# The third channel tile of a depthwise convolution, multiplied on ACT and added on POOL in turns with the fourth

## What is computed

```python
def causal_dwconv(u_ext, w, b):
    C = u_ext.shape[-1]
    y = lax.conv_general_dilated(u_ext, w[:, None, :], (1,), 'VALID',
                                 dimension_numbers=('NWC', 'WIO', 'NWC'), feature_group_count=C)
    return y + b

def conformer_conv(u, hist, conv_w, conv_b, ln_g, ln_b):
    ext = jnp.concatenate([hist, u], 1)
    y = jax.nn.silu(layernorm(causal_dwconv(ext, conv_w, conv_b), ln_g, ln_b))
    return y, ext[:, -(CONV_WIDTH - 1):]
```

## Time and profile before

| | before |
|---|---|
| median of 3 runs | 1135.22 us (1134.2 to 1147.78) |
| profiled execution, its own span | 1129.5 us |
| PE busy | 1068.1 us (95%) |
| DVE busy | 584.4 us (52%) |
| ACT busy | 395.1 us (35%) |
| POOL busy | 198.6 us (18%) |
| L1077 on DVE, 180 taps | 114.7 us |
| L638 on POOL, 30 adds | 50.3 us |

### The profile page before, as it was taken

How to read it: one execution, slowest core, us unless ns; L and a number is a source line. 1 busy time by engine, 2 the same in 40 slices (tenths; PEclk the granted TensorE clock), 3 DMA queues, 4 the chain that set the end, 5 groups by cost and what they waited for, 6 DMA issues and landing times.

```text
span 1129.5 us, 18024 instructions
## 1 busy us (share of the span) xinstructions
PE 1068.1 (95%) x6757; PEld 933.5 (83%) x6757; DVE 584.4 (52%) x1109; ACT 395.1 (35%) x683; POOL 198.6 (18%) x274
## 2 busy tenths in 40 slices
PE   4999966999999999999999969999999999999996
PEld 2999966767776667999998749999999999777774
DVE  4359599955543444233332274666666666311224
ACT  5111363332221313233221263455545554321212
POOL 6342364322221210001011000111111111000000
PEclk9999987899995955999999968999999999999998
DMA  6665332110000000223235301323222222332222
GB/s 191 156 181 168 67 66 60 57 34 2 1 1 1 1 1 1 76 74 93 74 92 160 105 19 57 92 75 92 74 86 81 87 80 74 93 84 80 75 75 84
DMA packets 110745, 83.93 MB, mean 74 GB/s; under 512 B 12962, under 2 KB 97834, under 8 KB 110632
## 3 DMA queue, kind: packets, MB, share of 16 engines
q1 hardware_dynamic: 104368, 65.64, 20.5%
q0 software_dynamic: 3904, 14.66, 4.7%
q10 hardware_dynamic: 2426, 2.98, 0.9%
HBM read 78.19 MB, written 7.18 MB: 76 GB/s over the span
## 4 chain that ended last, share of the span: by engine, by line
PE 87%; DVE 6%; DMA 2%; ACT 2%; issue 1%; POOL 1%; POOLq 0%; DVEq 0%; SPq 0%; ACTq 0%
PE ps L1405 21%; PE ps L1407 21%; PE ps L1406 21%; DVE yc L1077 4%; PE ps L1629 4%; PE ps L1472 3%; PE ps L1579 3%; PE ps L1610 2%; PE ps L1437 2%; PE ps L1582 2%; PE ps L1641 1%; PE ps L1627 1%; DMA page<-in_state_kv_win_dram 1%; PE ps L1584 1%; DMA x<-in_x_sample_dram 1%
## 5 line engine op out<-in xcount | busy, mean ns | idle before, releaser
L1405 PE MATMUL ps<-zh,wh 128*128 128x288 f32 (+1 forms) x1264 | 380.3, 301 | 21.5 <-DVE wl L1011 19.5
L1407 PE MATMUL ps<-zh,wl 128*128 128x288 f32 (+1 forms) x1264 | 378.1, 299 | 0.0
L1406 PE MATMUL ps<-zl,wh 128*128 128x288 f32 (+1 forms) x1264 | 378.1, 299 | 0.0
L1405 PEld LDWEIGHTS ps<-zh,wh 128*128 128x128 f32 (+1 forms) x1264 | 240.9, 191 | 23.6 <-DVE wl L1011 20.2
L1406 PEld LDWEIGHTS ps<-zl,wh 128*128 128x128 f32 (+1 forms) x1264 | 241.0, 191 | 0.9
L1407 PEld LDWEIGHTS ps<-zh,wl 128*128 128x128 f32 (+1 forms) x1264 | 240.6, 190 | 0.9
L1011 DVE TENSOR_TENSOR wl<-raw,wh 128x1024 fp32r<-128x1024 f32 (+1 forms) x49 | 59.1, 1205 | 183.9 <-ACT wh L706 183.6
L706 ACT CAST wh<-raw 128x1024 fp32r<-128x1024 f32 (+1 forms) x49 | 50.7, 1034 | 270.6 <-PE ps L1407 246.6
L1077 DVE SCALAR_TENSOR_TENSOR yc<-ext,par,yc 128x64 f32<-128x64 f32 (+1 forms) x180 | 114.7, 711 | 0.0
L968 ACT CAST wh<-raw 128x1024 fp32r<-128x1024 f32 x44 | 46.1, 1047 | 139.6 <-PE ps L1407 139.6
L849 ACT ACTIVATE probs<-ps,nmax 128x512 f32<-128x512 f32 (+5 forms) x76 | 39.4, 518 | 144.7 <-DVE nmax L1152 144.5
(11 more groups left out here) (256 smaller groups left out, 1605.8 us busy)
## 6 DMA issues: line engine op xcount, KB each, us to landing
raw<-in_w_up_dram SPq DMA_DIRECT2D x44, 512.0 KB, 3.9
raw<-in_w_in_dram SPq DMA_DIRECT2D x30, 512.0 KB, 3.9
raw<-in_w_down_dram SPq DMA_DIRECT2D x22, 512.0 KB, 3.8
page<-in_cache_kv_dram POOLq DMA_DIRECT2D x16, 256.0 KB, 3.0
raw<-in_w_out_dram SPq DMA_DIRECT2D x8, 512.0 KB, 3.8
x<-in_x_prompt_dram SPq DMA_DIRECT2D x4, 512.0 KB, 5.5
page<-in_state_kv_win_dram POOLq DMA_DIRECT2D x16, 128.0 KB, 2.9
raw<-in_w_in_dram SPq DMA_DIRECT2D x8, 256.0 KB, 3.5
```

Of the source, the lines that this page charges most:

```text
L1405: nc.tensor.matmul(out, ah, bh, start=start, stop=False)
L1406: nc.tensor.matmul(out, ah, bl, start=False, stop=False)
L1407: return nc.tensor.matmul(out, al, bh, start=False, stop=stop)
```

## The change

Tile 2 (the third) leaves DVE. ACT now makes, for each tap `l`, the product of tile 2 and then of tile 3, and POOL adds them in the same order. A product and its add have the number t = 2(l - 1) + h with h = 0 for tile 2 and 1 for tile 3, and take place t % 4 of the ring. One semaphore, `conv_23`, counts the adds of both. A product waits from t = 4 on until t - 3 adds are done, which frees its place. An add waits for its product and until t - 1 adds are done: with two tiles in turns that is the last add into its own tile, not the add straight before. DVE's tiles 0 and 1 keep their steps.

```diff
             for l in range(1, CW):
-                pool.wait_ge(conv_prod, 2 * (l + 1))
-                if l > 1:
-                    pool.wait_ge(conv_3, l - 1)
-                nc.gpsimd.tensor_tensor(yc[:, CT - 1, :], yc[:, CT - 1, :], cprod[:, l % 4, :], ALU.add)\
-                    .then_inc(conv_3, 1)
+                for h, c in enumerate((CT - 2, CT - 1)):
+                    t = 2 * (l - 1) + h
+                    pool.wait_ge(conv_prod, 2 * (2 * l + h + 1))
+                    if l > 1:
+                        pool.wait_ge(conv_23, t - 1)
+                    nc.gpsimd.tensor_tensor(yc[:, c, :], yc[:, c, :], cprod[:, t % 4, :], ALU.add)\
+                        .then_inc(conv_23, 1)
...
-                    if l >= 5:
-                        act.wait_ge(conv_3, l - 4)
-                    for part in range(2):
-                        w, src, dst = tap(CT - 1, l, part)
-                        if l == 0:
-                            nc.scalar.activation(dst, src, ACT.Identity, bias=par[:, P_CB + CT - 1:P_CB + CT],
-                                                 scale=w).then_inc(conv_prod, 1)
-                            continue
-                        prod = cprod[:, l % 4, 0:SEQ] if part == 0 \
-                            else cprod[:, l % 4, SEQ:NT].rearrange("p (b t) -> p b t", t=DT)
-                        nc.scalar.activation(prod, src, ACT.Copy, scale=w).then_inc(conv_prod, 1)
+                    for h, c in enumerate((CT - 2, CT - 1)):
+                        t = 2 * (l - 1) + h
+                        if t >= 4:
+                            act.wait_ge(conv_23, t - 3)
+                        for part in range(2):
+                            w, src, dst = tap(c, l, part)
+                            if l == 0:
+                                nc.scalar.activation(dst, src, ACT.Identity, bias=par[:, P_CB + c:P_CB + c + 1],
+                                                     scale=w).then_inc(conv_prod, 1)
+                                continue
+                            prod = cprod[:, t % 4, 0:SEQ] if part == 0 \
+                                else cprod[:, t % 4, SEQ:NT].rearrange("p (b t) -> p b t", t=DT)
+                            nc.scalar.activation(prod, src, ACT.Copy, scale=w).then_inc(conv_prod, 1)
...
-            act.wait_ge(conv_3, CW - 1)
+            act.wait_ge(conv_23, 2 * (CW - 1))
...
-                for done, tiles in ((conv_01, (0, 1)), (conv_2, (2,))):
-                    s0 = S_GLU + 2 * (tiles[-1] + 1)
-                    if s0 <= s < S_GATE:
-                        conv_taps(done, tiles, CW * (s - s0) // (S_GATE - s0), CW * (s + 1 - s0) // (S_GATE - s0))
+                s0 = S_GLU + 4
+                if s0 <= s < S_GATE:
+                    conv_taps(conv_01, (0, 1), CW * (s - s0) // (S_GATE - s0), CW * (s + 1 - s0) // (S_GATE - s0))
...
                             pe.wait_ge(conv_01, 4 * CW)
-                            pe.wait_ge(conv_2, 2 * CW)
-                            pe.wait_ge(conv_3, CW - 1)
+                            pe.wait_ge(conv_23, 2 * (CW - 1))
```

More of the change, by code:

```diff
@@ L321, in build_layer @@
         conv_01 = sem("conv_01")
-        conv_2 = sem("conv_2")
-        conv_3 = sem("conv_3")
+        conv_23 = sem("conv_23")
         conv_prod = sem("conv_prod")
```

## The result

| | before | changed |
|---|---|---|
| median | 1135.84 us (4 runs) | 1160.95 us (4 runs) |
| ratio | 1 | 1.0179, 95% interval 1.0104 to 1.0253 |
| the same again, in a later session | 1137.08 us (16 runs) | 1158.42 us (6 runs), ratio 1.022 (1.017 to 1.027) |
| profiled execution, span | 1129.5 us | 1155.5 us |
| L1520 / L1522 starts (compressed scores) | 205.53 us | 230.07 us |

The medians are over all runs, but the ratios and their intervals leave out the runs in a slower state of the chip, in which a program now and then finds itself (here one of the changed kernel's four, 1196.58 us). The changed kernel is slower, by 20 us by the ratio, 25 us between the medians and 26.0 us between the profiled spans. 32.6 were forecast. The measured ratio lies at the edge of 2%: the second, narrower interval is 1.7% to 2.7%.

What follows compares the result with a forecast made beforehand. PE bounds the kernel through L1520's start, which POOL's adds would set: 133.0 + 100.8 (56 adds at 1.80) + 2.5 + 1.8 = 238.1 us, 32.6 later. So 1135.2 + 32.6 = 1168 us, range 1151 to 1177.

Steps and rivals of the forecast that it cites:

- What bounds the kernel: Whole chain: mostly PE, with DVE in the convolution stretch; whatever moves L1520's start moves the end, with no later slack.
- DVE isn't relieved: Convolution from 128.9 us: 42 taps fewer save DVE 19 us, 30 more adds cost it 32 us.
- POOL becomes the bound, by the ring of four: Convolution stretch: ACT's last product waits for 56 adds, holding up the `ktok` copy and L1520; 14.4 us a step.
- The sum: First add to L1520: 144.5 + 52c for c us an add, so 238.1 us, + 32.6 us.
- First add: Start of POOL's adds: 131.8 us before, plus one more ACT pair of 1.15 us, gives 133.0.
- The hole: Step 12: ACT is away 9.7 us, four adds cover 7.2, so POOL is empty for 2.5 us.
- The pace: POOL's adds beside DVE's taps: 1.80 us an add, gap of 0.14 left in; 56 adds take 100.8 us.
- The last pair and the copy: End of the convolution: last pair 0.97 us, `ktok` copy to L1520 0.92, less 0.1 overlap, 1.8 us.
- The chances: Whole kernel: slower by over 2% 0.85, within 2% 0.12, faster 0.03.
- Rival A: POOL's adds run at nearly their own pace, 1.40 to 1.60 us; 1147 to 1157 us; chance 0.12.
- Rival B: DVE's relief decides: PE's 19.5 us of waiting come back, the kernel gets faster, 1116 us; chance 0.03.
- Rival C: DVE and POOL take turns by whole instructions: 2.01 us an add, + 44, 1179 us; chance 0.10 including beyond the main case.

Runs made afterwards that it cites:

- the trial with the relief alone: Kernel before, with the third tile's 42 DVE taps from step 10 on left out and nothing in their place; 1120.59 us, ratio 0.9873.
- the trial with the old wait: Changed kernel, but each POOL add again waits for the add straight before it; 1169.57 us, ratio 1.034 to the kernel before.
- the second division of the taps: Kernel before, all work kept, with more DVE taps in steps 4, 8, 9 and fewer in steps 10 to 15; 1123.88 us, ratio 0.9904.

## Why the prediction was right, and by how much it was off

*What bounds the kernel.* Right. The start of L1520 carried 24.5 of the 26.0 us, and nothing later gave it back. That nothing behind it changes was right to 1.5 us: the 40 transposes of L1439 (L1437 before) start at 666.90 before and 692.90 after, 26.0 later, and L1581 24.5 later. The 1.5 us come in at one place. The tenth of DVE's reductions into `nmax` starts at 256.72 before and 281.21 after, 24.5 later; the eleventh at 259.40 and 285.47, 26.1 later, and so it stays. Just there PE's granted clock fell in the changed kernel (the window's last three figures are clock, DMA share and GB/s):

```profile
280.00:295.00 15.00, 15.00 (x90) 10.86 (x90) 9.24 (x24) 3.45 (x10) 3.07 (x4) 0.89 0.01 2
```

The kernel before is at 1.00 from 250 to 325 us. That the stretch from L1522 to L1581 kept its length (26.2 after 26.3) is in part luck: when the changed kernel was run again, L1522 started at 230.08 and L1581 at 257.54, 27.5 later.

*DVE isn't relieved.* Right. From 128.9 us on I had 84.6 + 32 - 19 = 97.6 us of taps, and DVE was busy with its 72 taps for 95.57 us. That makes (95.57 - 72 x 0.46) / 60 = 1.04 us of DVE per add where I had 1.1. What the working missed is how little of the 19 us would have reached PE: the trial with the relief alone has about 10.

*POOL becomes the bound, by the ring of four.* Right. ACT waits 24.4 us in 42 places, and POOL's only hole is the one at step 12.

*The sum.* 238.1 us was said for L1522, and it started at 230.07. Term by term:
- First add: 133.0 said, 132.53 measured.
- The hole: 2.5 said, 3.47 measured. A quicker pace empties the ring sooner, as the term 9.7 - 4c says (3.1 for 1.65).
- The pace: 1.80 said, 1.648 measured, 8.5 us over 56 adds. This is the mis-sized term, the step "I leave it in, and put it in the range". I saw that an add may follow the one before last, and held that closing the gap only moves the wait where a tap uses it. The trial with the old wait has 1.754: so 5.9 of the 8.5 us are that relaxed wait, and the other 2.6 are that 1.80 was a little high even with the old wait; what made it so was not tested. The gap is where the second of two short taps slipped in. Without it that tap takes a turn of its own, which costs DVE and saves POOL.
- The last pair and the copy: 1.8 both times.

*The chances.* Slower by over 2% was given 0.85. The measurement puts it at 1.8% and, repeated, at 2.2%, so it is not decided on which side of the limit it lies. By the prediction's own sum the limit is passed at 1.61 us an add, and the pace of 1.648 came out just beyond it; at 1.80 it would have been clear. The range, 1151 to 1177, holds 1161.

*Rival A* (1.40 to 1.60 us an add) was right in its reason, since the relaxed wait did give POOL its next turn sooner, and too strong in its number: a long tap between two adds still costs POOL 0.45 us (144.30, 145.69 and 147.53 are starts of adds; the first two are 1.39 apart and the next 1.84). *Rival B* is ruled out by the adds alone. *Rival C,* the whole instructions one after the other, would have 2.01 us an add for three adds and four taps, and the trial with the old wait, which has that mixture, shows 1.754. In the changed kernel there is one tap to an add, for which whole instructions would make 1.40 + 0.46 = 1.86, and the trace has 1.648. Either way what one engine adds to the other's turn is less than its own time alone. The Trainium skill (SBUF — State Buffer, Who interferes with whom) has the blocked engine wait for the whole instruction of the other: the trace agrees for DVE, whose blocked taps end after the add, and not for the sum of both, which comes out under that of the whole instructions.

## What to carry to other kernels

Before work is moved from DVE to POOL, read what one POOL instruction costs DVE while both run: here 1.0 to 1.1 us for each add. So a 512 and a 64 column tap, 0.92 us of DVE, were replaced by an add that cost DVE at least as much. Count then the receiver's instructions times its shortest recorded duration against the stretch in which they have to fit; the shortest add of the kernel before took 1.395 us, and 56 x 1.395 = 78 us against 73.7 said no before anything was run. Count as relief only what stands ahead of the last wait that it is to shorten: here 20 of 42 taps. And look for idle time of the loaded engine ahead of the contended stretch: the 12 us that DVE waited there were worth more than a second engine.

## What was not expected of the hardware

**One instruction per add.** Where POOL's next add was ready before the last had ended, DVE got exactly one instruction per add (58 steps of 58), whatever its size: a 64-column tap takes 0.27 us alone and 1.43 to 1.47 in its turn, a 512-column tap 0.74 and 1.9. The `wl` subtractions, 1.21 us each before, took 2.44 in three cases of six. So beside these adds a short tap lost the most for its size, 1.16 us on 0.27, where a long one lost as much on 0.74.

**A part of a gain goes back through TensorE's clock.** The kernel that is 15.0 us earlier at the attention loses most of that in its profiled execution, whose span of 1127.1 us is only 2.4 under the kernel before's. In windows of the attention (length, busy us (count) of PE, PEld, DVE, ACT, POOL, granted clock, DMA), the kernel before:

```profile
300.00:312.00 12.00, 12.00 (x86) 9.09 (x85) 8.32 (x24) 3.65 (x11) 3.30 (x5) 1.00 0.01 3
```

and the one with the second division of the taps:

```profile
285.00:306.00 21.00, 21.00 (x87) 14.93 (x87) 8.79 (x24) 3.66 (x11) 3.33 (x5) 0.55 0.01 2
```

Windows with the same 24 DVE and 11 ACT instructions are 12 us long at a granted clock of 1.00 (2.4 GHz) and 21 us at 0.55 (near 1.2 GHz). PE was busy throughout both windows and for 29.94 of the 30 us ahead of each. Each kernel has such a fall later in the attention (the kernel before 0.50 from 340 to 355 us). This one comes on top in the profile of the second division. In the one with the third tile's taps left out it stands in place of a later one: 14.5 us ahead at the attention's start, that kernel is 16.9 ahead at the end. The changed kernel has only the short one before 355 us (0.89 from 280 to 295). That the lower clock costs the time is shown by the windows. What lowered it is open: the convolution stretch ahead, in which PE had waited less, is what differs, but no run tests it, and the profiled execution was among the longer ones of its kernel.
